# Exponents of a gated linear recurrence: matmuls against step tables, or a running sum and subtractions on GpSimd

## The reference

```python
def hgrn2_chunk(S, q, k, v, logf):
    b = jnp.cumsum(logf, axis=1)
    inter = jnp.einsum('blhk,bhkv->blhv', q * jnp.exp(b), S)
    diff = b[:, :, None] - b[:, None, :]
    dec = jnp.exp(jnp.where(causal[None, :, :, None, None], diff, -jnp.inf))
    A = jnp.einsum('blhk,bmhk,blmhk->bhlm', q, k, dec)
    intra = jnp.einsum('bhlm,bmhv->blhv', A, v)
    bl = b[:, -1]
    k_dec = k * jnp.exp(bl[:, None] - b)
    S_new = jnp.exp(bl)[..., None] * S + jnp.einsum('blhk,blhv->bhkv', k_dec, v)
    return S_new, intra + inter
```

## Time and profile before

| | us |
|---|---|
| median of 3 runs (1228.81 to 1230.55) | 1229.45 |
| the profiled execution | 1232.34 |
| its span, first to last instruction | 1230.6 |
| TensorE busy (89% of the span) | 1095.6 |
| VectorE busy (58%) | 708.4 |
| ScalarE busy (49%) | 602.1 |
| GpSimd busy (9%) | 107.1 |
| the four rounds of the mixers lie at about | 70 to 640 |

### The profile page before, as it was taken

How to read it: one execution, slowest core, us unless ns; L and a number is a source line. 1 busy time by engine, 2 the same in 40 slices (tenths; PEclk the granted TensorE clock), 3 DMA queues, 4 the chain that set the end, 5 groups by cost and what they waited for, 6 DMA issues and landing times. The chain is left out here.

```text
span 1230.6 us, 26353 instructions
## 1 busy us (share of the span) xinstructions
PE 1095.6 (89%) x8820; PEld 898.8 (73%) x8821; DVE 708.4 (58%) x1321; ACT 602.1 (49%) x1226; POOL 107.1 (9%) x237
## 2 busy tenths in 40 slices
PE   4789999999999999999949999549999998999936
PEld 3688788977898778977837878337877776777722
DVE  3623555245632565326645665777886674767538
ACT  5634445334553444534453212156876664767433
POOL 0000000000000000000000011120011001100150
PEclk9799999999999999999969999659999999999978
DMA  8632222141222321223226341369999996999565
GB/s 308 226 92 74 80 83 60 36 141 53 67 70 58 95 79 35 65 74 118 83 69 212 103 155 60 127 207 338 394 388 351 319 332 229 365 311 350 188 246 205
DMA packets 202399, 210.53 MB, mean 171 GB/s; under 512 B 15612, under 2 KB 169076, under 8 KB 202036
## 3 DMA queue, kind: packets, MB, share of 16 engines
q1 hardware_dynamic: 183120, 177.25, 43.4%
q0 software_dynamic: 5712, 18.23, 4.1%
q10 hardware_dynamic: 13492, 13.96, 3.2%
HBM read 185.32 MB, written 24.08 MB: 170 GB/s over the span
## 5 line engine op out<-in xcount | busy, mean ns | idle before, releaser
L2019 DVE TENSOR_TENSOR experts_w_lo<-all_raw_more,experts_w_hi 128x2048 fp32r<-128x2048 f32 x48 | 108.4, 2287 | 7.2 <-ACT experts_w_hi L1900 7.2
L2019 DVE TENSOR_TENSOR experts_w_lo<-all_raw,experts_w_hi 128x2048 fp32r<-128x2048 f32 x48 | 109.6, 2284 | 4.9 <-ACT experts_w_hi L1900 4.9
L923 PE MATMUL early_ps_proj<-early_w_hi,early_h_hi 128*128 128x512 f32 x256 | 106.4, 416 | 2.6 <-ACT mixers_decay L756 2.6
L2187 PE MATMUL experts_ps_g<-experts_w_hi,experts_x_hi 128*128 128x512 f32 x256 | 104.5, 408 | 2.2 <-DVE experts_x_lo L2025 2.2
L925 PE MATMUL early_ps_proj<-early_w_hi,early_h_lo 128*128 128x512 f32 x256 | 101.2, 395 | 0.0
L2189 PE MATMUL experts_ps_g<-experts_w_hi,experts_x_lo 128*128 128x512 f32 x256 | 100.9, 394 | 0.0
L924 PE MATMUL early_ps_proj<-early_w_lo,early_h_hi 128*128 128x512 f32 x256 | 100.6, 393 | 0.0
L2188 PE MATMUL experts_ps_g<-experts_w_lo,experts_x_hi 128*128 128x512 f32 x256 | 100.5, 393 | 0.0
L1196 DVE TENSOR_TENSOR mixers_qd_t<-mixers_turned,early_tables 128x128 f32<-128x128 f32 (+1 forms) x36 | 10.1, 281 | 152.7 <-ACT mixers_turned L804 135.4
L1900 ACT ACTIVATE experts_w_hi<-all_raw 128x2048 fp32r<-128x2048 f32 x48 | 91.5, 1911 | 5.2 <-DMA all_raw<-in_W_up_e_dram 4.7
L1900 ACT ACTIVATE experts_w_hi<-all_raw_more 128x2048 fp32r<-128x2048 f32 x48 | 91.6, 1913 | 2.0 <-DMA all_raw_more<-in_W_up_e_dram 1.4
(11 more groups left out here) (358 smaller groups left out, 2687.9 us busy)
## 6 DMA issues: line engine op xcount, KB each, us to landing
all_raw_more<-in_W_down_e_dram SPq DMA_DIRECT2D x128, 256.0 KB, 5.4
all_raw<-in_W_gate_e_dram SPq DMA_DIRECT2D x96, 256.0 KB, 5.4
all_raw<-in_W_up_e_dram SPq DMA_DIRECT2D x96, 256.0 KB, 6.5
all_raw<-in_W_in_dram SPq DMA_DIRECT2D x32, 512.0 KB, 4.9
all_raw<-in_W_ada_dram SPq DMA_DIRECT2D x32, 512.0 KB, 4.7
condition_w_ada_in<-in_W_ada_dram SPq DMA_DIRECT2D x4, 2048.0 KB, 12.7
all_raw_more<-in_W_gate_e_dram SPq DMA_DIRECT2D x32, 256.0 KB, 7.2
all_raw_more<-in_W_up_e_dram SPq DMA_DIRECT2D x32, 256.0 KB, 7.3
```

Source lines behind the costliest of these rows:

```text
L923: pe.matmul(out, xhi, whi, start=(k == 0), stop=False)
L2019: dve.tensor_tensor(w_lo[:, 2 * p:2 * p + 2], raw_pair[p], f32(w_hi[:, 2 * p:2 * p + 2]), ALU.subtract).then_inc(lo_done, 1)
L2187: pe.matmul(out, x_hi[:, k, :], w_hi[:, c, at], start=(k == 0), stop=False)
```

## The change

Nothing of the exponents is left on TensorE. VectorE replaces log f by its running sum, in place, by a scan of each of the nine tiles, once per round, after the logarithm. GpSimd subtracts within a tile, channels on the partitions: one instruction for plane 0 and two for each level, one for the half of every block ahead of the middle and one for the half behind it, with the operands in opposite order so that every exponent is at most zero. They fill a new SBUF tile `span`, which has one buffer. ScalarE takes the exponentials from `log_f` and `span`. `turn_log`, `log_high`, `log_low`, `exponents`, the table `steps` with its transfer and its cast are gone, and with them the wait L980 and the wait L914.

```diff
-    between = lambda ref: ((m > ref) & (m <= l)) | ((m > l) & (m <= ref))
-    c["steps"] = np.stack([m > l, *(between(l // (2 * h) * (2 * h) + h - 1) for h in LEVELS), m <= l], 1)
...
-        steps = sb("steps", [P, 9, P], F32R)
-        lf_hi = sb("lf_hi", [P, P], F32R)
-        lf_lo = sb("lf_lo", [P, P], F32R)
+        span = sb("span", [P, 8, P])
...
+                def spans(i):
+
+                    w = frames(i)
+                    pool.wait_ge(sum_done, n[9] + (i + 1))
+                    pool.wait_ge(exp_done, n[9] + i)
+                    b = log_f[:, at(i):at(i) + w]
+                    pool.tensor_tensor(span[:, 0, 0:w], b[:, w - 1:w].broadcast_to([P, w]), b, ALU.subtract)
+                    for c, h in enumerate(LEVELS, 1):
+                        if 2 * h > w:
+                            continue
+                        pairs = b.rearrange("p (b l) -> p b l", l=2 * h)
+                        out = span[:, c, 0:w].rearrange("p (b l) -> p b l", l=2 * h)
+                        middle = pairs[:, :, h - 1:h].broadcast_to([P, w // (2 * h), h])
+                        pool.tensor_tensor(out[:, :, 0:h], middle, pairs[:, :, 0:h], ALU.subtract)
+                        last = pool.tensor_tensor(out[:, :, h:2 * h], pairs[:, :, h:2 * h], middle, ALU.subtract)
+                    last.then_inc(level_done, 1)
+
+                spans(0)
                 for i in range(NT + 2):
                     if i >= 2:
                         refine(i - 2)
+                    if i + 1 < NT:
+                        spans(i + 1)
...
                 def decays(i):
                     w = frames(i)
-                    act.wait_ge(d_done, n[9] + (i + 1))
+                    act.wait_ge(level_done, n[9] + (i + 1))
                     act.wait_ge(kl_done, n[9] + i)
                     act.wait_ge(ql_done, n[9] + i)
-                    act.activation(decay[:, 8, 0:w], ps_cum[:, 0:w], ACT.Exp)
-                    act.activation(decay[:, 4:8, 0:w], ps_d[:, :, 0:w], ACT.Exp)
-                    front = ps_p[(i + 1) % 2].rearrange("p (c l) -> p c l", l=P)
-                    for lo, hi in [(0, 4)] if w == P else [(0, 1), (3, 4)]:
-                        last = act.activation(decay[:, lo:hi, 0:w], front[:, lo:hi, 0:w], ACT.Exp)
+                    act.activation(decay[:, 8, 0:w], log_f[:, at(i):at(i) + w], ACT.Exp)
+                    for lo, hi in [(0, 8)] if w == P else [(0, 1), (3, 8)]:
+                        last = act.activation(decay[:, lo:hi, 0:w], span[:, lo:hi, 0:w], ACT.Exp)
                     last.then_inc(exp_done, 1)
...
-                            pe.wait_ge(exp_done, n[9] + 1)
...
-                    pe.wait_ge(exp_done, n[9] + min(i + 2, NT))
...
-            dve.wait_ge(fetched, 16)
-            dve.tensor_copy(steps[:, :, :], decay[:, :, :]).then_inc(cleared, 1)
...
+                def run(i):
+
+                    f = log_f[:, at(i):at(i) + frames(i)]
+                    dve.tensor_tensor_scan(f, s.const("ones", 0, frames(i)), f, 0.0, ALU.mult, ALU.add)\
+                       .then_inc(sum_done, 1)
...
-                log_low(0)
+                dve.wait_ge(logf_done, n[1] + 1)
+                for i in range(NT):
+                    run(i)
```

72 lines of the change are left out of this document (10 added, 62 removed).

## The result

The changed kernel takes 1244.95 us (median of 4 runs, 1241.53 to 1246.12), the kernel before 1230.0 us (median of 4). The ratio is 1.0105, with a 95% interval from 1.0077 to 1.0133: about 1% slower. Measured again beside later experiments it was 1244.26 against 1230.85 us, 1.0094 (1.0078 to 1.0111). The forecast was 1247 us.

A forecast was written before the change was run, and what follows sets the result against it. It took TensorE and a ScalarE-VectorE loop of 10.2 us as two limits of the same length. Per round -1.0 + 5.0 - 0.8 + 1.3 = +4.5, four rounds +18 us, so 1247 us; 8 in 10 from 1213 to 1278.

The forecast's parts named there:

- The loop beside TensorE: Mixer tiles: ScalarE and VectorE release each other once per tile, a loop of 10.2 us that closes without TensorE.
- Rival 3: Mixers: the loop is not rigid and TensorE was the bound; up to -43 us, 1186; chance 0.06 with partial forms.
- two equal limits: Mixer tiles: TensorE and the ScalarE-VectorE loop both limit at 10.2 us; taking work from one leaves the other.
- What GpSimd costs by itself: GpSimd in each tile: 0.30 us a subtraction, 4.6 us for fifteen, hidden with 4 us to spare.
- rival 4's first part: GpSimd becomes the bound if a strided subtraction takes 0.5 us or more; 1275 to 1290; chance 0.20 for both parts.
- What GpSimd costs VectorE: VectorE's two-SBUF-input instructions wait for GpSimd: 1.0 us per interval in five intervals, +5.0 us a round.
- the 0.20 us of `log_low`: ScalarE-VectorE loop: `log_low` leaves, 0.20 us gained in each of five intervals, -1.0 us a round.
- The start of a round: Tile 1's exponentials wait for GpSimd; TensorE idles 4.5 us, then 2.0 us lost to half clock; +1.3 us.
- Tile 4: Interval with `condition`, 11.92 us before: TensorE comes 1.35 us earlier, the loop needs 11.1 us; -0.8 us.
- rival 4: GpSimd becomes the bound, 1275 to 1290, or TensorE's clock falls, 0.4 us per tile, 1258; chance 0.20 for both.
- The sum: Whole kernel: -1.0 + 5.0 - 0.8 + 1.3 = +4.5 us a round, +18 us over four rounds.

The follow-up runs named there:

- e2_copy_first: Changed kernel with ScalarE's copy of the sample tile's turned rows put ahead of tile 1's exponentials once a round; 1225.91 us, ratio 0.9941.
- e9_stores_late: Changed kernel with the two DMA starts of the sample state's stores moved on ScalarE from behind tile 3 to behind tile 8; 1237.34 us, ratio 1.004.
- e3_two_of_15: Changed kernel with only two of GpSimd's fifteen subtractions made for tiles 2 to 8, results not the reference's; 1252.6 us, a total that can't be used.
- e4_fill: Changed kernel with ten useless matmuls put on TensorE in each of tiles 1 to 8, ahead of turning the normalised outputs; 1236.08 us, ratio 1.0031.
- e8_before_copy_first: Kernel before with ScalarE's copy of the sample tile's turned rows put ahead of tile 1's exponentials in each round; 1236.39 us, ratio 1.0049.
- e1_two_spans: Changed kernel with two buffers for the differences, so tile 1's are made ahead of the round's first exponential; 1228.16 us, ratio 0.9964.

## Why the prediction came out as it did

The side was right and the time 2 us off, but in good part by luck: single terms were wrong by more than that in both directions and cancelled, and a part of the time came from stages that the forecast had at nothing.

**The loop beside TensorE.** Right for tiles 3, 6, 7 and 8: filling TensorE there changed nothing, and taking the exponents away did not either. Rival 3 (TensorE was the bound, -43 us) is out for this order of the queues. But the picture of two equal limits was too even. At the turn and in tile 4 the kernel before was TensorE's, by at least 3.5 us (the turn of e2_copy_first) and 1.5 us (tile 4 of e9_stores_late), and the shared bank tied ScalarE's exponentials to TensorE's scores, which I had not seen as part of the loop.

**What GpSimd costs by itself.** I took 0.30 us for a subtraction and 4.6 for fifteen. The rows have 0.29 with starts 0.25 apart, and 0.40 for the wide one: 4 us, or 6 with the two that are stretched. It was hidden in the tiles, with 3.2 us to spare (181.19 is GpSimd's next instruction). Strided halves were no dearer, so rival 4's first part is out.

**What GpSimd costs VectorE.** The mechanism was right and its size wrong. I had 1.0 us per interval in five; it is 0.43 us in three, tiles 3, 6 and 7. GpSimd was quicker than I took it to be, so that few of its instructions were left for VectorE's run, and each meeting costs VectorE 0.1 us, where I had 0.16 and six of them. The term was +5.0 a round; it is +1.3. Against it stand the 0.20 us of `log_low`, confirmed by the intervals of 9.99 in e3_two_of_15 against 10.19.

The Trainium skill ("SBUF — State Buffer", section on SBUF's two separate sides) has the shared port pair as an exclusive lock for the whole instruction. For GpSimd the trace agrees: its instructions of 1.14 and 1.27 us end within 0.2 us of VectorE's. For VectorE it agrees only in part: L1088 starts 0.23 us before GpSimd's instruction ends, and is 0.10 longer than alone. The Trainium skill's 4497 ns for 2048 elements ("GPSIMD Engine Reference", section on performance versus the Vector engine) give 0.14 us for 64 elements as an estimate; here starts lie 0.25 apart, so a fixed share comes on top that counts at this size.

**The start of a round.** I had +1.3 and the turn is 1.26 longer, again by errors that cancelled. Counted from ScalarE's first instruction on the projection of the sample frames (249.90 before, 251.21 after), I had TensorE get on after 8.8 us; it was 7.9, since it stood still 3.2 us and not 4.5. From there to the copy I had 10.1 us of work at full clock and 2.0 for the clock; by e4_fill the work is 10.6, and the clock cost 2.5 (13.10 us in all, 259.15 to 272.25). So 0.9 too much stands against 1.0 too little. That the clock would be at 0.50 for some six microseconds was right (257.9 to 264.7). I had named the mechanism, and missed that it was worth curing: the copy of tile 0 need not have stood behind the wait, and one swap of order brings 19 us.

**Tile 4.** I had -0.8, from a loop of 11.1 us. It is 0.0. The loop is 10.4 (e3, e4, e9), which would have been -1.5; the idle stretch of 2.75 us ahead of it and the clock took that back. The fall of the clock in the tiles stood in rival 4 with 0.4 us in each. It came in one tile of the round, behind the longest wait of the tiles, and in the fourth round in tile 8 too, behind 1.90 us. The length of a single wait does not settle it: 2.4 us ahead of tile 8 left the clock at 1.00 in three rounds of the changed kernel and were followed by a fall in three rounds of e9_stores_late, and in e8_before_copy_first the wait of 1.63 us at the turn was followed by one in three rounds and not in the third. In e1_two_spans one came behind 1.73 us, in tile 7 of the third round.

**The sum.** Forecast +4.5 a round and +18 in all; measured +1.7 a round, +2.5 more in the fourth, 9.0 in the mixers, and 3.6 in the experts that nobody had forecast. So of 18 us half was there. The rest of the measured 15 came from elsewhere: 3.6 us from the experts, and 2.3 since the profiled execution before (1232.34) lay above its median (1230.0).

## What to carry over

When work leaves an engine that looks bound, go along the whole period and ask at each wait what TensorE does while it waits: where it becomes idle for some microseconds (here 1.6 to 3.2), its clock may fall and take a second toll (here 1.1 to 2.5 us), which can be as large as what was moved away. An experiment that takes one such wait away may only move the fall to the next one, so read the clock of every round beside the times. Then look at the order of the queues again; an order that was right while the work was there (a copy behind the exponentials) can be the wrong one afterwards, and the shared bank or buffer that forced it may be gone. Price a move with the old order kept and with the order fitted to it: here the same move is +1% in the one and -1.9% in the other (-1.5% against the kernel before with the same two DMA starts moved).

## What the hardware did that I had not expected

- Useless matmuls made a kernel faster, 1244 to 1236 us, mostly by keeping the granted clock at 1.00 in two places of each round and in tile 8 of the fourth; 1.7 of the 8 us are a DMA start that was short.
- The same wait of 2.4 us ahead of tile 8 left the clock at 1.00 in three rounds of one kernel and was followed by a stretch at 0.50 in three rounds of another, 1.1 us of the tile's time.
- VectorE loses only about 0.1 us at a meeting with GpSimd, while GpSimd's instruction is stretched from 0.29 to 1.27 us.
- A DMA start on ScalarE's queue took 2.10 and 1.79 us in the fourth round of two profiles of the same kernel and 0.41 in the other rounds, and held the squares behind it.
- Stops of 2.2 to 5.4 us on TensorE in an unchanged stage, in all ten profiles of the one family but at most 0.2 us in the four of the other.
